# Reversing the moving operand and the PSUM write of the 512-column fp32r matmuls

## What is computed

```python
def hybrid_layer(x, p_i, ...):
    h = rmsnorm(x, norm_mix)
    z = h @ w_in                      # 1024 x 3336
    ...                               # retention, causal pooling and mLSTM on slices of z
    x = x + jnp.concatenate([y_ret, y_pool, y_ml], axis=-1) @ w_out
    h = rmsnorm(x, norm_ffn)
    gu = h @ w_gate_up                # 1024 x 5632
    x = x + (jax.nn.silu(gu[..., :D_FF]) * gu[..., D_FF:]) @ w_down
    hp = rmsnorm(x, norm_ple)
    x = x + jax.nn.sigmoid(hp @ w_ple_gate) * (p_i @ w_ple_proj)
    return x
```

## Time and profile before

| | us |
|---|---|
| median of 3 runs | 2496.57 |
| lowest and highest run | 2496.37, 2498.0 |
| span of the profiled execution | 2494.5 |
| TensorE matmuls busy | 2467.6 |
| TensorE weight loads busy | 2037.2 |
| VectorE, ScalarE, GpSimd busy | 1270.7, 898.2, 992.5 |

### The profile page before, as it was taken

One profiled execution on the slowest core, in us unless ns is written; L12 is line 12 of the kernel. 1 busy time (PEld: TensorE's weight loads), 2 busy tenths in 40 slices (PEclk: granted clock), 3 DMA queues, 4 the chain that ended last, 5 costly groups with the idle time before them and its releaser, 6 DMA issues.

```text
span 2494.5 us, 29698 instructions
## 1 busy us (share of the span) xinstructions
PE 2467.6 (99%) x11768; PEld 2037.2 (82%) x11768; DVE 1270.7 (51%) x1760; ACT 898.2 (36%) x1298; POOL 992.5 (40%) x596
## 2 busy tenths in 40 slices
PE   7999999999999999999999999999999999999998
PEld 6888888888888888888878887888888888888886
DVE  7967845543343352333596777545433433423335
ACT  4333334433333341125333252344433333322253
POOL 3211112278877832321221121223788877222120
PEclk9999999999999999999999999999999999999999
DMA  4342222123223252211143322311232223422111
GB/s 164 105 98 65 71 85 85 45 84 92 76 77 91 87 195 107 78 50 44 38 154 98 78 56 67 102 59 60 80 93 81 76 85 110 150 110 70 51 49 70
DMA packets 89370, 214.43 MB, mean 86 GB/s; under 512 B 34568, under 2 KB 43016, under 8 KB 84880
## 3 DMA queue, kind: packets, MB, share of 16 engines
q1 hardware_dynamic: 61456, 126.90, 16.9%
q10 hardware_dynamic: 27776, 85.63, 10.0%
HBM read 163.70 MB, written 35.68 MB: 80 GB/s over the span
## 4 chain that ended last, share of the span: by engine, by line
PE 97%; DVE 1%; ACT 1%; issue 0%; DMA 0%; POOL 0%; ACTq 0%; DVEq 0%; POOLq 0%
PE proj L1986 20%; PE proj L1987 20%; PE proj L1988 20%; PE proj L2090 5%; PE aux L2090 5%; PE aux L2089 5%; PE proj L2089 5%; PE aux L2088 5%; PE proj L2088 5%; PE aux L2205 1%; PE aux L2224 1%; PE aux L2215 1%; PE aux L2310 0%; PE aux L2315 0%; PE aux L2281 0%; PE aux L2268 0%
## 5 line engine op out<-in xcount | busy, mean ns | idle before, releaser
L1937 POOL TENSOR_TENSOR w_lo<-w_raw,w_hi 128x1024 fp32r<-128x1024 f32 (+1 forms) x144 | 367.2, 2551 | 1256.5 <-ACT w_hi L1468 1256.4
L1986 PE MATMUL proj<-h_hi,w_hi 128*128 128x512 f32 x1760 | 694.8, 395 | 0.9 <-POOL w_lo L1937 0.9
L1988 PE MATMUL proj<-h_lo,w_hi 128*128 128x512 f32 x1760 | 685.5, 389 | 0.0
L1987 PE MATMUL proj<-h_hi,w_lo 128*128 128x512 f32 x1760 | 685.1, 389 | 0.0
L1986 PEld LDWEIGHTS proj<-h_hi,w_hi 128*128 128x128 f32 x1760 | 330.4, 188 | 72.4 <-issue 3.1
L1988 PEld LDWEIGHTS proj<-h_lo,w_hi 128*128 128x128 f32 x1760 | 330.3, 188 | 69.2
L1987 PEld LDWEIGHTS proj<-h_hi,w_lo 128*128 128x128 f32 x1760 | 330.5, 188 | 68.8 <-issue 2.4
L1468 ACT ACTIVATE w_hi<-w_raw 128x1024 fp32r<-128x1024 f32 (+1 forms) x143 | 146.5, 1026 | 440.5 <-PE proj L1988 295.9
L1025 DVE TENSOR_TENSOR x<-x,proj 128x512 f32<-128x512 f32 x128 | 87.7, 687 | 405.6 <-PE proj L1988 405.3
L1944 POOL TENSOR_TENSOR w_lo<-w_raw,w_hi 128x512 fp32r<-128x512 f32 x120 | 183.5, 1531 | 88.5 <-ACT w_hi L1450 88.5
L1944 POOL TENSOR_TENSOR w_lo<-turns,w_hi 128x512 fp32r<-128x512 f32 x120 | 180.4, 1504 | 62.9 <-ACT w_hi L1450 62.9
(11 more groups left out here) (290 smaller groups left out, 4161.3 us busy)
## 6 DMA issues: line engine op xcount, KB each, us to landing
w_raw<-weights SPq DMA_DIRECT2D x168, 512.0 KB, 3.7
act_spill<-act ACTq DMA_DIRECT2D x44, 512.0 KB, 5.5
turns<-weights SPq DMA_DIRECT2D x40, 512.0 KB, 4.4
h_whole<-act_spill ACTq DMA_DIRECT2D x12, 1024.0 KB, 8.1
ffn_b_whole<-act_spill ACTq DMA_DIRECT2D x8, 1024.0 KB, 5.5
w_raw<-weights SPq DMA_DIRECT2D x16, 384.0 KB, 3.1
ml_d<-rows_spill ACTq DMA_DIRECT2D x64, 64.0 KB, 3.4
rows<-ret_qkv ACTq DMA_DIRECT2D x32, 128.0 KB, 2.3
```

Source lines behind the costliest of these rows:

```text
L1937: g.tensor_tensor(wlo[:, slot, 0:n], w, whi[:, slot, 0:n].bitcast(F32), ALU.subtract).then_inc(weights_ready.sem, 1)
L1986: pe.matmul(out, wh, rhi, start=first, stop=False)
L1987: pe.matmul(out, wl, rhi, start=False, stop=False)
L1988: return pe.matmul(out, wh, rlo, start=False, stop=final)
```

## The change

A helper returns its tensor with the columns in reverse, as an access pattern with a step of -1. It is applied to the output and to both moving operands of `three_passes`, and to the output and both moving operands of `product_of`. Input column 511 is read first and output column 511 is written first; every column keeps its place in memory on both sides. The stationary operands, `two_passes` and all other matmuls are as before.

```diff
+            def turned(tokens):
+                return tokens[:, ::-1]
+
             def three_passes(out, slot, col, rhi, rlo, first, final):
 
                 wh, wl = whi[:, slot, col:col + P], wlo[:, slot, col:col + P]
+                out, rhi, rlo = turned(out), turned(rhi), turned(rlo)
                 pe.matmul(out, wh, rhi, start=first, stop=False)
                 pe.matmul(out, wl, rhi, start=False, stop=False)
                 return pe.matmul(out, wh, rlo, start=False, stop=final)
...
                 wh, wl = operand_slot(L, b, i)
+                out = turned(out)
                 turn = {M_S2: 0, M_S1: 1, M_S3: 2, M_A22: 3}
...
-                    hi, lo = moving(i, j)
+                    hi, lo = [turned(t) for t in moving(i, j)]
                     o = slice(P * j, P * j + P)
                     pe.matmul(out, wh[:, o], hi, start=first and j == 0, stop=False, skip_group_check=True)
                     pe.matmul(out, wl[:, o], hi, start=False, stop=False, skip_group_check=True)
```

## The result

The changed kernel takes 2560.4 us (median of 4 runs, 2560.1 to 2562.01) against 2496.5 us for the kernel before: a ratio of 1.0255, 95% interval 1.024 to 1.0269. It is slower by 63.9 us.

What follows compares the result with a forecast made beforehand. TensorE's matmuls were taken to bound the kernel, 10080 changed ones at 226.7 ns each; every term was zero, so the 2494.5 us span stayed, giving 2496.6 us as run median, range 2485 to 2520.

Steps and rivals of the forecast that it cites:

- Step (1): Instructions of the changed kernel: same matmuls, loads and waits in the same order, only start address and step sign differ; zero.
- Step (2): Successive passes into one PSUM bank: each column is still rewritten one step, 226.7 ns, after its last write; cost zero.
- step (3): Reading and writing downwards on the changed matmuls: the unknown, bounded by half pace above and 135 us off below; taken as zero.
- Step (5): Other engines read the banks forward as before, and their waits are slack behind TensorE; cost zero.
- Which value I take: zero: Value chosen for downward reading and writing: same words and aligned lines as forward, so no added time per matmul.
- Step (4): Weight loads, one per changed matmul: they follow the matmuls' cadence and stay hidden, 109 against 226.7 ns; cost zero.
- a fixed cost per instruction: Rival: each turned matmul's start or turn costs some cycles, 4.2 us per cycle, up to 135 us; chance 0.06 beyond 5 us.
- Small amounts are likelier than large ones: Judgement on extra start cycles per turned matmul: one cycle is 4.2 us in all, six are 25 us.
- The half rate: Rival: turned fp32r streams move one column every two cycles, giving about 4521 to 4546 us; chance 0.18.
- The 13.4 ns "something else": Part of each forward 226.7 ns step above the 213.3 ns that 512 columns need at 2.4 GHz, unexplained.

Runs made afterwards that it cites:

- the stream: Bare streams of matmuls, the kernel's whole computation left out, operand order or weight placement varied by section; 512 fp32r columns forward took 226.6 ns, read turned 233.5.

## Why the prediction was wrong

I forecast no change, 2496.6 us, in a range of 2485 to 2520; it was 2560.4.

Step (1), no instruction added, held: the counts are equal. Step (2), no cost from the dependence between passes, held, and the write side of step (3) with it: turning the writes alone gives 0.9999. Step (5), the other engines don't matter, held.

The step that failed is the value in (3), "Which value I take: zero", for the reading side. I argued that a turned stream fetches as many words from the same lines and that no row makes -4 slower than +4. The number of words is indeed the same, and turning inside a word is indeed free. What I left out is that words are fetched next to a second stream, the weight load, and that order and placement of words within 256 bytes matter. It measures 6.67 ns a matmul, 63.9 us in all.

Step (4) failed in part. The weight loads don't set the cadence, but "cost zero" treated them as bystanders. Two streams from one memory that always ran in one fixed relation was what the earlier trace rows showed, and the only pace I had was the pace in that relation.

The mechanism is nearest to the rival "a fixed cost per instruction", to which I gave 0.06. Its bounds were right (up to 13.4 ns, 135 us) and its term was mis-sized: the range allowed 5.6 cycles of 2.4 GHz and it is 16. "Small amounts are likelier than large ones" had no row behind it. Nor was it quite a fixed cost: at 256 columns there is none. I held against it that plain fp32 shows only 3.3 ns over its columns. That row could not speak on this: the stream shows plain fp32 unaffected by turning (429.1 ns both ways). The half rate, with 0.18 the strongest rival, fell too: no form with a step of -1 ran at half the rate.

The 13.4 ns "something else" in the forward step was the hint. I named it and made it the bound; the runs resolve it into 2.5 ns that remain even when only one word is read (215.8 - 213.3) and 10.9 ns that come with reading the whole tile.

**Shown:** the cost is on the read side and per matmul. Of the cases run, fp32r at full clock has it at 512 and 384 columns and not at 256, and bf16, plain fp32 and fp32r at the low clock don't. It depends on the order of 16-byte words within 256 bytes, and the pace, forward and turned, also depends on how the moving tile and the weights lie to each other. **Open:** what in SBUF or TensorE the two reads share; why a shorter load or weights from one column don't free the read; why one form can hold two paces (240.0 or 233.3 ns turned, 226.7 or 233.5 forward at 16 bytes), depending, it seems, on what ran before. That the two reads get in each other's way is the reading that fits, and no view shows the collision itself. No run has a falling weight read, which would tell whether two falling streams fit each other again.

## What to carry to other kernels

Where a kernel is bound by fp32r matmuls of 512 columns, keep the moving tile and the weight tile at the same offset modulo 256 bytes (16 bytes off was as good in one stream and 5 to 7 ns a matmul worse in another) and read the moving operand in rising order within each 256 bytes; a stray 64-byte tile ahead of the weights cost this kernel 2.5%. Reversals are free on the PSUM side, inside a 16-byte word and by whole blocks of 256 bytes, so do them there. When a forecast of "no change" rests on one pace, ask in which relations of address that pace has been seen at all.

## What the runs showed of the hardware that I had not expected

- The mean steps of fp32r matmuls of 512 columns gathered at multiples of 8 cycles of 1.2 GHz: 226.7, 233.3 and 240.0 ns are 272, 280 and 288 cycles. They are means: in the kernel with weights 64 bytes further on, half of the block products' steps are at 229 to 232 ns and half at 235 to 238. Other forms lay between (228.9, 231.8, 236.6 ns). The worst order found, 16 columns turned inside each 64 bytes, took 266.6 ns, 320 cycles, at each of four shifts.
- The kernel before has the placement (shift 0) that was the best of sixteen in the stream, and it is a narrow one: 32 bytes to either side cost 6.6 to 6.7 ns a matmul there.
- Two words read by turns (8 columns over and over) ran at 216.6 ns, but four at 242.0 and eight at 236.6; from sixteen on it was 226.6 to 227.3. Reading fewer different words isn't faster by itself.
- A step of 2 over fp32r columns, 256 of them, took 229.8 ns against 119.9 with a step of 1, although two of four columns of each 16-byte word were used; in bf16 the same step cost only 113.3 against 109.7. On the write side a step of 2 took 214.9 ns for 256 bf16 columns in place of 109.7.
